# Seven-product FFN pairs added up in PSUM, with two plain tiles in place of three, and whole 128-row blocks at x

## The chip, the cores and the metric

The kernel runs on one core of a Trainium2 chip. The metric is the device time of one execution in microseconds. The kernel before has a median of 978.66 us over 3 runs (978.25 to 978.79); the profiled execution took 978.82 us, and its span, from the first to the last instruction, is 977.0 us.

## The reference

One layer of a streaming encoder on 512 prompt rows and 64 sample rows (576 rows in all, width 1024). After RMSNorm one wide projection feeds attention and retention; their merged output goes through an output projection and is added to x. Then come the FFN and a small per-layer input:

```
h = rmsnorm(x, g_ffn_pre)
f = (jax.nn.silu(h @ w_ffn_gate) * (h @ w_ffn_up)) @ w_ffn_down
x = x + rmsnorm(f, g_ffn_post)
x = x + (p @ w_ple_proj) * jax.nn.sigmoid(x @ w_ple_gate)
```

Everything is in float32. The hidden width of the FFN is 2816, which is 22 tiles of 128, called f tiles.

## The kernel before

Activations are held transposed: 128 features on the partitions, the 576 rows as columns, worked on in two halves of 288. Each float32 product is made of three matmuls in a reduced type. Every operand is split in a high part (a rounded copy, by ScalarE) and a low part (the operand less the high part, by VectorE), and PSUM adds high x high, high x low and low x high. One such `triple` (L970) is three matmuls of 128x128 by 128x288. Weights go from HBM to `raw`, ScalarE makes `whi` (function `hi`), VectorE makes `wlo` (function `lo`), and TensorE waits for `lo_ready`.

*At the start.* x arrives with its rows on the partitions, in five blocks: four of 128 rows, and one of the 64 sample rows. `x_transposes(k)` (L770) turns 128 features of all five blocks; the last transpose is of 64 rows. There are eight such groups for x, two for p, and one like it in `row_factor` (L751). Between them run the first units of the projection. ScalarE makes `xh` from PSUM, VectorE makes `xl` and the copy `x_t`.

*The FFN.* An f tile needs a gate and an up product. The first three f tiles (`PLAIN`) are plain: gate and up are units `("ffn", n)`, each of 8 k tiles and 2 halves, 96 matmuls in all for an f tile. The other 19 are *pairs*: gate and up of one f tile are the two halves of a block product done with seven products in place of eight (a Strassen-Winograd form). Each product is of 4 k tiles, so a pair has 84 matmuls. The factors on the side of the activations are parts of `yh`, `yl`, or differences of them: `t_sum` (VectorE) forms four differences of 4x288 columns, `t_high` (ScalarE, L1490) and `t_low` (VectorE, L2152) split them into `th` and `tl`. They are made once, before the first pair. The factors on the side of the weights are quarters of the loaded weights or sums of them: `sum_of` (VectorE, L2189) writes `s_sum`, then `hi` and `lo` split it. PA0, PA1, PB1 and the like name the seven products; each has a PSUM bank of its own. What comes out is added by VectorE in SBUF: `u_sums`, `gate_sum`, `up_late` and `f_out` hold seven additions of 288 columns and the final product of 576. ScalarE copies only the first product (`kept`), and does the SiLU. The function `product_out` is what ScalarE and VectorE do once product t of pair i is done; part of it is operand t of pair i+1.

*The order* is written out by hand, engine by engine: an engine does its list in order, and each step waits for counters of the others. `bank_turns` numbers the uses of each PSUM bank; `open_bank` on TensorE waits until the use before has been read (`bank_read`). Behind the first units ("ffn", 0) to ("ffn", 3) TensorE goes on with units 4 and 5, which are the third plain tile, then with the pairs. Meanwhile ScalarE and VectorE finish f of the tiles 0 and 1 (`gate_silu`, `f_half`, `f_half_low`), make the `t` factors, and with `first_products` the operands of the first pair.

Of the kernel before, what the change touches and what calls it, by code (L numbers as in the profile page):

```python
# [14 lines left out]
P = 128  # L15
# [126 lines left out]
def block_size(b):  # L142
# [4 lines left out]
    if b == RH:  # L147
# [5 lines left out]
PLAIN = 3  # L153
# [4 lines left out]
FFN_BANK = {(0, 0): 0, (1, 0): 1, (2, 0): 2, (3, 0): 3, (0, 1): 0, (1, 1): 4, (2, 1): 5, (3, 1): 1,  # L158
            (4, 0): 2, (4, 1): 3, (5, 0): 4, (5, 1): 5}
PA0, PS1, PS2, PA1, PS4, PS3, PB1 = range(PRODUCTS)  # L160
# [98 lines left out]
def bank_turns():  # L259
# [3 lines left out]
    used = [0] * PRODUCTS  # L263
    n = 0
    for e in EVENTS:
        if e[0] == "prod":
            b = e[2]
        else:
            if e in (("down", 0, 0), ("down", KD, 0), ("down", 2 * KD, 0)):
                n = 0  # L270
# [21 lines left out]
S_STEP = {PS1: 0, PS2: 1, PS4: 2, PS3: 3}  # L292


def encoder_layer(nc, x_p, x_s, p_p, p_s, cache_k, cache_v, state_in, g_mix_pre, w_in, sinks_in,
                  w_ba, w_br, w_out, g_mix_post, g_ffn_pre, w_fg, w_fu, w_fd, g_ffn_post, w_pp, w_pg,
                  table_in, scratch, y_p, y_s, k_p, v_p, r_p, k_s, v_s, r_s):
    with ExitStack() as ctx:
# [228 lines left out]
        banks = [acc[:, b // 2, b % 2, 0:HALF] for b in range(4)] + [small[:, 512 * b:512 * b + HALF] for b in range(3)]  # L527
# [161 lines left out]
        def _(pe):  # L689
# [61 lines left out]
            def row_factor(n):  # L751

                pe.wait_ge(rstd_ready, n + 1)
                for r in range(RT):
                    size = P if r < RT - 1 else DEC
                    ins = nc.tensor.transpose(small[:, r * P:r * P + size], rstd[0:size, r:r + 1].to_broadcast([size, P]),
                                              ident[0:size, 0:size])
                ins.then_inc(bcast_done, 1)
# [11 lines left out]
            def x_transposes(k):  # L770

                if k < KD:
# [6 lines left out]
                for r in range(RT):  # L779
                    size = P if r < RT - 1 else DEC  # L780
                    ins = nc.tensor.transpose(small[:, at + r * P:at + r * P + size],
                                              src[0:size, r, col:col + P], ident[0:size, 0:size])
# [191 lines left out]
            def triple(e, weights, x_h, x_l, first, last):  # L974

                (w_h, w_l), bank = weights, bank_of(e)
                nc.tensor.matmul(bank, w_h, x_h, start=first, stop=False)  # L977
                nc.tensor.matmul(bank, w_h, x_l, start=False, stop=False)  # L978
                return nc.tensor.matmul(bank, w_l, x_h, start=False, stop=last)  # L979

            def open_bank(e):
# [3 lines left out]
                elif b == PB1:  # L985
                    pe.wait_ge(yn_ready, 2 * KD)
# [108 lines left out]
            def product(i, t):  # L1095
# [7 lines left out]
                for k in range(KD // 2):  # L1103
                    ins = triple(e, weight(e, k), x_h[:, k, :], x_l[:, k, :], k == 0, k == KD // 2 - 1)
                done(ins, e)

            def f_wait(i):

                pe.wait_ge(f_lo, (3, 4, 6)[i] if i < PLAIN else PLAIN + i + 1)
# [50 lines left out]
        def _(act):  # L1160
# [344 lines left out]
            hi(("ffn", 4))  # L1505
            hi(("ffn", 5))
# [9 lines left out]
            def first_products(i, n):


                for t in ((PA0, PS1), (PS2, PA1), (PS4, PS3), (PB1,))[n]:
                    hi(("prod", i, t))  # L1520

            for n in range(3):
                first_products(PLAIN, n)
            gate_silu(2, 0)
            gate_silu(2, 1)
            first_products(PLAIN, 3)
            f_half(2, 0)
            f_half(2, 1)
# [6 lines left out]
            def f_high(i):  # L1535

                act.wait_ge(f_ready, i - PLAIN + 1)
                nc.scalar.activation(fh[:, i - GROUPS[group_of(i)][0], :], ta[:, :], ACT.Copy).then_inc(f_hi, 1)

            def product_out(i, t, first, last):  # L1540
# [11 lines left out]
                if t == PS3:  # L1552
# [113 lines left out]
        def _(dve):  # L1666
# [499 lines left out]
            lo(("ffn", 4))  # L2166
# [397 lines left out]
```

## Time and profile before

| what | value |
|---|---|
| median of 3 runs | 978.66 us |
| profiled execution | 978.82 us |
| its span | 977.0 us |
| TensorE busy | 969.8 us, 99% |
| VectorE busy | 632.0 us, 65% |
| ScalarE busy | 397.6 us, 41% |
| TensorE in the chain that ended last | 98% |
| granted TensorE clock | 1.00 |

Busy time counts an engine as working when any of its instructions runs; matmuls overlap their neighbours in the pipe, so the time from one start to the next is the cost of a matmul and not its duration. A wait row names the engine that waits, what it was about to do, and who released it.

### The profile page before, as it was taken

The numbers are of one execution on the slowest core, as the hardware profiler recorded it, in microseconds if no ns is written. First come the engines' busy times: TensorE is split into PE (matmuls) and PEld (weight loads), VectorE is DVE, ScalarE is ACT, GpSimd is POOL, SyncE is SP. The second block draws the span as 40 slices with busy tenths as digits, with TensorE's granted clock in tenths as the row PEclk, the third lists the DMA queues.
The fourth block names the chain that finished last, engine by engine and source line by source line (L and its number), as shares of the span: only waits on it lengthen the run. The fifth ranks groups of instructions, "written<-read, shape, count | busy, mean of one in ns | idle before, by whom it ended". The sixth has DMA issues, their size and how long they took to land.

```text
span 977.0 us, 18648 instructions
## 1 busy us (share of the span) xinstructions
PE 969.8 (99%) x7263; PEld 950.6 (97%) x7263; DVE 632.0 (65%) x1248; ACT 397.6 (41%) x699; POOL 85.9 (9%) x140
## 2 busy tenths in 40 slices
PE   8999999999999999999999999999999999999998
PEld 7999999999999999999999999999999999999997
DVE  5554676757665643435458899525997469976772
ACT  5333533434343522223455555424453234543352
POOL 2123212122100000010003000000000000030000
PEclk9999999999999999999999999999999999999999
DMA  8534221222122222246604533521334213356221
GB/s 216 147 110 131 80 61 55 66 76 70 58 69 66 76 88 86 76 124 174 195 4 119 205 87 87 152 65 46 109 102 122 79 44 106 105 188 207 87 55 44
DMA packets 166244, 98.67 MB, mean 101 GB/s; under 512 B 14688, under 2 KB 162560, under 8 KB 165904
## 3 DMA queue, kind: packets, MB, share of 16 engines
q1 hardware_dynamic: 159936, 79.19, 28.5%
q0 software_dynamic: 4336, 16.67, 4.9%
q10 hardware_dynamic: 1888, 1.64, 0.6%
q8 instruction: 58, 0.95, 0.4%
q14 instruction: 26, 0.21, 0.1%
HBM read 86.79 MB, written 10.75 MB: 100 GB/s over the span
## 4 chain that ended last, share of the span: by engine, by line
PE 98%; DMA 1%; DVE 0%; SPq 0%; ACT 0%; issue 0%; DVEq 0%; ACTq 0%
PE acc L697 37%; PE acc L977 11%; PE acc L978 11%; PE acc L979 11%; PE small L977 6%; PE small L978 6%; PE small L979 6%; PE small L846 1%; PE small L892 1%; PE small L863 1%; PE small L896 1%; PE small L855 1%; PE small L894 1%; DMA x_row<-in_x_sample 1%; PE acc L808 1%; PE small L877 1%
## 5 line engine op out<-in xcount | busy, mean ns | idle before, releaser
L697 PE MATMUL acc<-xh,whi 128*128 128x288 f32 x720 | 158.6, 301 | 0.1
L697 PE MATMUL acc<-xh,wlo 128*128 128x288 f32 x720 | 153.4, 294 | 0.0
L697 PE MATMUL acc<-xl,whi 128*128 128x288 f32 x720 | 153.4, 294 | 0.0
L1166 ACT ACTIVATE whi<-raw 128x1024 fp32r<-128x1024 f32 (+1 forms) x60 | 60.1, 1001 | 197.6 <-PE acc L697 196.0
L697 PEld LDWEIGHTS acc<-xh,whi 128*128 128x128 f32 x720 | 114.0, 188 | 5.8 <-issue 4.7
L697 PEld LDWEIGHTS acc<-xh,wlo 128*128 128x128 f32 x720 | 115.0, 188 | 0.0
L697 PEld LDWEIGHTS acc<-xl,whi 128*128 128x128 f32 x720 | 114.9, 188 | 0.0
L2008 DVE TENSOR_TENSOR wlo<-raw,whi 128x512 fp32r<-128x512 f32 (+2 forms) x93 | 81.0, 872 | 51.2 <-ACT whi L1387 35.5
L977 PE MATMUL acc<-yh,whi 128*128 128x288 f32 x360 | 107.0, 297 | 0.0
L979 PE MATMUL acc<-yh,wlo 128*128 128x288 f32 x360 | 106.1, 295 | 0.0
L1675 DVE TENSOR_TENSOR wlo<-raw,whi 128x1024 fp32r<-128x1024 f32 (+1 forms) x62 | 71.8, 1158 | 44.2 <-ACT whi L1166 43.4
L977 PE MATMUL acc<-fh,whi 128*128 128x288 f32 x264 | 77.9, 295 | 0.0
L978 PE MATMUL acc<-fl,whi 128*128 128x288 f32 x264 | 77.8, 295 | 0.0
L978 PE MATMUL acc<-yl,whi 128*128 128x288 f32 x264 | 77.7, 294 | 0.0
L979 PE MATMUL acc<-fh,wlo 128*128 128x288 f32 x264 | 77.7, 294 | 0.0
L1395 ACT ACTIVATE whi<-s_sum 128x512 fp32r<-128x512 f32 x76 | 47.7, 630 | 61.5 <-DVE s_sum L2189 50.9
L977 PEld LDWEIGHTS acc<-yh,whi 128*128 128x128 f32 x360 | 67.6, 188 | 0.0
L979 PEld LDWEIGHTS acc<-yh,wlo 128*128 128x128 f32 x360 | 67.6, 188 | 0.0
L1711 DVE TENSOR_TENSOR zt<-acc,rb 128x576 f32<-128x576 f32 x40 | 30.3, 756 | 52.3 <-PE acc L697 52.3
L2008 DVE TENSOR_TENSOR wlo<-s_sum,whi 128x512 fp32r<-128x512 f32 x76 | 51.7, 683 | 8.6 <-ACT whi L1395 8.6
L1387 ACT ACTIVATE whi<-raw 128x1024 fp32r<-128x1024 f32 (+1 forms) x38 | 38.2, 1011 | 40.8 <-PE acc L979 18.1
L978 PEld LDWEIGHTS acc<-yl,whi 128*128 128x128 f32 x264 | 49.6, 188 | 0.0
(337 smaller groups left out, 2392.2 us busy)
## 6 DMA issues: line engine op xcount, KB each, us to landing
raw<-in_w_in SPq DMA_DIRECT2D x91, 256.0 KB, 3.2
raw<-in_w_ffn_gate SPq DMA_DIRECT2D x44, 256.0 KB, 3.4
raw<-in_w_ffn_up SPq DMA_DIRECT2D x44, 256.0 KB, 4.1
raw<-in_w_ffn_down SPq DMA_DIRECT2D x32, 256.0 KB, 3.4
res<-x_scratch POOLq DMA_DIRECT2D x16, 288.0 KB, 4.3
raw<-in_w_branch_ret SPq DMA_DIRECT2D x16, 256.0 KB, 3.1
raw<-in_w_out SPq DMA_DIRECT2D x16, 256.0 KB, 4.3
raw<-in_w_ffn_down SPq DMA_DIRECT2D x16, 192.0 KB, 3.5
```

The lines of the kernel that those rows point to most:

```text
L697: ins = nc.tensor.matmul(acc[:, a, hf, 0:HALF], w[:, s, at:at + P], x(k)[:, hf * HALF:(hf + 1) * HALF], start=first and n == 0 and m == 0, ...
L808: ins = nc.tensor.matmul(acc[:, 0, hf, 0:HALF], w[:, at], x[:, k, hf * HALF:(hf + 1) * HALF], start=k == 0 and m == 0, stop=k == KD - 1 an ...
L846: ins = nc.tensor.matmul(att[0:nq, slot * KW + k0:slot * KW + k1], q_st[64 * g:64 * g + 64, 2 * p + j, 0:nq], k_st[64 * g:64 * g + 64, k0: ...
L977: nc.tensor.matmul(bank, w_h, x_h, start=first, stop=False)
L978: nc.tensor.matmul(bank, w_h, x_l, start=False, stop=False)
L979: return nc.tensor.matmul(bank, w_l, x_h, start=False, stop=last)
L1166: nc.scalar.activation(whi[:, s, 0:n], raw[:, s, 0:n], ACT.Copy).then_inc(hi_ready, 1)
L1387: nc.scalar.activation(dst[:, 0:n], raw_of(RAW[u])[:, 0:n], ACT.Copy).then_inc(hi_ready, 1)
L1395: nc.scalar.activation(dst[:, 0:QUART], s_sum[:, S_STEP[u[2]], :], ACT.Copy).then_inc(hi_ready, 1)
L1675: nc.vector.tensor_tensor(wlo[:, s, 0:n], raw[:, s, 0:n], whi[:, s, 0:n].bitcast(F32), ALU.subtract).then_inc(lo_ready, 1)
L1711: nc.vector.tensor_tensor(halves(dst), acc_of(a), halves(rb[:, :]), ALU.mult).then_inc(acc_free[a], 1)
L2008: nc.vector.tensor_tensor(dst[:, 0:n], src[:, 0:n], high[:, 0:n], ALU.subtract).then_inc(lo_ready, 1)
```

## The change

1. `PLAIN` is 2: f tile 2 becomes a pair, the units ("ffn", 4) and ("ffn", 5) go.
2. Within a pair, products that are summed go to one PSUM bank and are added up there: PA0, then PS2, PS3 and PB1 on top (bank 0 of the pair's three), PS1 and on top of it PS4 (bank 2), PA1 alone (bank 1). Pairs take the banks 0 to 2 and 3 to 5 in turn. What is needed of a sum on its way is copied out by ScalarE before TensorE adds the next one: PA0, PS1 and PS2. VectorE keeps three additions of 288 columns (`add_kept`), and the final product is in two pieces of 288 columns, one of them read straight from PSUM. PS3 now comes before PS4.
3. In front of the first pair, the lists of ScalarE and VectorE are set again: the first pair's operands come between the `t` factors, and with the first pair the operands of the second come two products later (`OPERANDS_AT`).
4. At x, p and the row factor, the block of 64 sample rows is transposed as a block of 128 rows, whose other rows GpSimd has set to zero.

```diff
-PLAIN = 3
+PLAIN = 2
...
-PA0, PS1, PS2, PA1, PS4, PS3, PB1 = range(PRODUCTS)
+PA0, PS1, PS2, PA1, PS3, PS4, PB1 = range(PRODUCTS)
+OPERANDS_AT = ([[t] for t in range(PRODUCTS)],
+               [[], [], [PA0], [PS1], [PS2], [PA1, PS3], [PS4, PB1]])
+PAIR_BANK = {PA0: 0, PS2: 0, PS3: 0, PB1: 0, PA1: 1, PS1: 2, PS4: 2}
+ADDED = (PS2, PS3, PB1, PS4)
...
-            b = e[2]
+            b = PAIR_BANK[e[2]] + 3 * ((e[1] + PLAIN) % 2)
...
             def x_transposes(k):
+                pe.wait_ge(rows_padded, 1 if k < KD else 2)
...
-                    size = P if r < RT - 1 else DEC
-                    ins = nc.tensor.transpose(small[:, at + r * P:at + r * P + size],
-                                              src[0:size, r, col:col + P], ident[0:size, 0:size])
+                    ins = nc.tensor.transpose(small[:, at + r * P:at + (r + 1) * P], src[:, r, col:col + P], ident)
...
-            for n in (4, 5):
-                for h in range(2):
-                    half_unit("ffn", n, h, yh, yl)
...
-                    ins = triple(e, weight(e, k), x_h[:, k, :], x_l[:, k, :], k == 0, k == KD // 2 - 1)
+                    ins = triple(e, weight(e, k), x_h[:, k, :], x_l[:, k, :], k == 0 and t not in ADDED,
+                                 k == KD // 2 - 1, t in ADDED)
...
-                if t == PA0:
-                    copy_out(e, kept[:, 0, :])
+                if t in (PA0, PS1, PS2):
+                    copy_out(e, kept[:, (PA0, PS1, PS2).index(t), :])
...
-                    hi(("prod", i + 1, t))
+                    for n in OPERANDS_AT[i == PLAIN][t]:
+                        hi(("prod", i + 1, n))
...
+            def add_kept(i, t, dst, n):
+                e, copied = ("prod", i, t), ("prod", i, (PA0, PS1, PS2)[n])
+                dve.wait_ge(bank_read[BANK[copied]], TURN[copied] + 1)
+                dve.wait_ge(pe_done, EVENT[e])
+                nc.vector.tensor_tensor(dst, bank_of(e), kept[:, n, :], ALU.add).then_inc(bank_read[BANK[e]], 1)
...
+            nc.gpsimd.memset(x_row[DEC:P, RT - 1, :], 0.0).then_inc(rows_padded, 1)
+            nc.gpsimd.memset(p_row[DEC:P, RT - 1, :], 0.0).then_inc(rows_padded, 1)
```

How the lists stand in front of the first pair is seen best in the built programs. VectorE before, from the third `t_sum` to the first pair's first low part (`wlo_128<-raw_126` at the end; `ta<-...,tb` is `f_half`, `fl` is `f_half_low`, `tl` is `t_low`, and `wlo<-raw` 128x1024 is the low part of ("ffn", 5)):

```order
L2145 TENSOR_TENSOR t_high_part<-wide 128x1152
L2141 SCALAR_TENSOR_TENSOR t_high_part<-t_low_part,wide 128x1152
L2008 TENSOR_TENSOR wlo<-raw,whi 128x1024
L2127 TENSOR_TENSOR ta<-small,tb 128x288
L2132 TENSOR_TENSOR fl<-ta,fh 128x288
L2152 TENSOR_TENSOR tl<-t_low_part,th 128x1152 x2
L2127 TENSOR_TENSOR ta<-acc,tb 128x288
L2132 TENSOR_TENSOR fl<-ta,fh 128x288
L2189 TENSOR_TENSOR s_sum<-raw_126 128x512
L2008 TENSOR_TENSOR wlo_128<-raw_126,whi_127 128x512
```

VectorE in the change, from the same step:

```order
L2140 TENSOR_TENSOR t_high_part<-wide 128x1152
L2136 SCALAR_TENSOR_TENSOR t_high_part<-t_low_part,wide 128x1152
L2122 TENSOR_TENSOR ta<-small,tb 128x288
L2127 TENSOR_TENSOR fl<-ta,fh 128x288
L2147 TENSOR_TENSOR tl<-t_low_part,th 128x1152
L2122 TENSOR_TENSOR ta<-acc,tb 128x288
L2180 TENSOR_TENSOR s_sum<-raw 128x512
L2003 TENSOR_TENSOR wlo<-raw,whi 128x512
L2180 TENSOR_TENSOR s_sum<-s_sum,raw 128x512
L2003 TENSOR_TENSOR wlo<-s_sum,whi 128x512
L2147 TENSOR_TENSOR tl<-t_low_part,th 128x1152
```

Two low parts of 1024 columns are gone (one stands just ahead of these rows), the second `tl` now comes behind the first pair's first operands, and so does a `fl`.

ScalarE before, from the first two `t_high` to the copy of the first product (`kept<-acc`); `tb` is the SiLU of a plain tile, `fh` the high part of f, `whi<-s_sum` and `whi<-raw` 128x512 are operands of the first pair:

```order
L1490 ACTIVATE th<-t_low_part 128x1152 x2
L1479 ACTIVATE tb<-small 128x288
L1485 ACTIVATE fh<-ta 128x288
L1490 ACTIVATE th<-t_high_part 128x1152 x2
L1392 ACTIVATE whi_127<-raw_126 128x512
L1395 ACTIVATE whi_127<-s_sum 128x512 x2
L1392 ACTIVATE whi_127<-raw_126 128x512
L1395 ACTIVATE whi<-s_sum 128x512 x2
L1479 ACTIVATE tb<-acc 128x288 x2
L1392 ACTIVATE whi<-raw_126 128x512
L1485 ACTIVATE fh<-ta 128x288 x2
L1533 ACTIVATE kept<-acc 128x288
```

ScalarE in the change, from the same step:

```order
L1488 ACTIVATE th<-t_low_part 128x1152 x2
L1477 ACTIVATE tb<-small 128x288
L1483 ACTIVATE fh<-ta 128x288
L1390 ACTIVATE whi<-raw 128x512
L1393 ACTIVATE whi<-s_sum 128x512
L1488 ACTIVATE th<-t_high_part 128x1152
L1393 ACTIVATE whi<-s_sum 128x512
L1390 ACTIVATE whi<-raw 128x512
L1488 ACTIVATE th<-t_high_part 128x1152
L1393 ACTIVATE whi_127<-s_sum 128x512 x2
L1390 ACTIVATE whi_127<-raw 128x512
L1525 ACTIVATE kept<-acc 128x288 x3
```

The first pair's high parts now stand between the `th` in place of behind them, and the SiLU and `fh` of the third plain tile are gone. The copy of the first product, now with those of the second and third, stands behind all seven high parts of its pair, as it did before. What is new is that TensorE waits for it: PS2 is opened by `bank_read` of the bank that the copy reads.

## Rows read from the trace of the kernel before

**Rows 1.** The profile's page, parts 1 and 4: busy time by engine; shares of the ending chain.

```profile
PE 969.8 (99%) x7263; PEld 950.6 (97%) x7263; DVE 632.0 (65%) x1248; ACT 397.6 (41%) x699; POOL 85.9 (9%) x140
...
PE 98%; DMA 1%; DVE 0%; SPq 0%; ACT 0%; issue 0%; DVEq 0%; ACTq 0%
```

**Rows 2.** The waits of TensorE: what it waited for, us in total, times, longest; first and last.

```profile
PE small L781 <- DMA x_row<-in_x_sample: 1.6, 2, 0.8
...
PE acc L764 <- DVE rowsum L1686: 1.1, 1, 1.1
```

**Rows 3.** Windows: last plain tile, first pair: length, busy (instructions) by engine, clock, DMA.

```profile
549.87:562.62 12.75, 12.75 (x98) 12.75 (x97) 9.56 (x14) 7.92 (x12) 0.00 (x0) 1.00 0.24 67
562.62:573.74 11.12, 11.12 (x86) 11.12 (x85) 10.63 (x19) 5.34 (x12) 0.00 (x0) 1.00 0.23 66
```

**Rows 4.** Timeline of VectorE before the first pair: start us, us, line, operation, count, idle before.

```profile
550.42 1.22 DVE L2008 TENSOR_TENSOR wlo<-raw,whi 128x1024 fp32r<-128x1024 f32 x1
551.56 0.45 DVE L2127 TENSOR_TENSOR ta<-small,tb 128x288 f32<-128x288 f32 x1
...
553.58 2.63 DVE L2152 TENSOR_TENSOR tl<-t_low_part,th 128x1152 fp32r<-128x1152 f32 x2 [0.60 <-ACT th L1490]
556.12 0.45 DVE L2127 TENSOR_TENSOR ta<-acc,tb 128x288 f32<-128x288 f32 x1
...
559.71 0.69 DVE L2008 TENSOR_TENSOR wlo<-raw,whi 128x512 fp32r<-128x512 f32 x1 [1.57 <-ACT whi L1392]
```

**Rows 5.** Timeline of ScalarE before the first pair, the same columns.

```profile
552.04 0.45 ACT L1485 ACTIVATE fh<-ta 128x288 fp32r<-128x288 f32 x1 [6.30 <-DVE ta L2127]
552.39 2.21 ACT L1490 ACTIVATE th<-t_low_part 128x1152 fp32r<-128x1152 f32 x2
554.50 0.39 ACT L1479 ACTIVATE tb<-small 128x288 f32<-128x288 f32 x1
556.61 0.45 ACT L1485 ACTIVATE fh<-ta 128x288 fp32r<-128x288 f32 x1 [1.71 <-DVE ta L2127]
556.96 2.20 ACT L1490 ACTIVATE th<-t_high_part 128x1152 fp32r<-128x1152 f32 x2
...
559.59 0.62 ACT L1395 ACTIVATE whi<-s_sum 128x512 fp32r<-128x512 f32 x1
...
565.82 0.41 ACT L1533 ACTIVATE kept<-acc 128x288 f32<-128x288 f32 x1
```

**Rows 6.** Timeline of TensorE's weight loads at one block of x, by form.

```profile
12.29 0.49 PEld L781 LDWEIGHTS small<-tab,x_row 128*128 128x128 f32 x4
12.95 0.14 PEld L781 LDWEIGHTS small<-tab,x_row 64*128 64x128 f32 x1 [0.17 <-issue]
```

**Rows 7.** Windows on TensorE: one block at x, and the two at p.

```profile
18.40:19.13 0.73, 0.73 (x7) 1.00 0.90 362
28.00:29.52 1.52, 1.52 (x12) 1.00 0.53 104
```

**Rows 8.** Timeline of TensorE behind the block of 18.40.

```profile
19.13 0.53 PE L697 MATMUL acc<-xh,whi 128*128 128x288 f32 x2
19.50 0.43 PE L697 MATMUL acc<-xl,whi 128*128 128x288 f32 x2
```

**Rows 9.** Timeline of ScalarE in the first projection unit.

```profile
14.30 1.06 ACT L1166 ACTIVATE whi<-raw 128x1024 fp32r<-128x1024 f32 x1 [0.29 <-DMA raw<-in_w_in]
```

**Rows 10.** Timeline of TensorE: the matmul behind that low part, and the row factor.

```profile
16.71 0.53 PE L697 MATMUL acc<-xh,whi 128*128 128x288 f32 x2
...
34.41 0.79 PE L756 MATMUL small<-tab,rstd 128*128 128x128 f32 x5
```

**Rows 11.** Timeline of GpSimd: the row factor's power.

```profile
32.72 1.21 POOL L2395 TENSOR_TENSOR rstd<-rowvar,neg_half 128x5 f32<-128x5 f32 x1 [14.03 <-DVE rowvar L1681]
```

**Rows 12.** Timeline of TensorE: the same matmul of ones at the start and later.

```profile
1.11 4.10 PE L764 MATMUL acc<-ones 128*128 128x128 f32 x20 [1.11 <-DVE rowsum L1686]
...
7.76 1.38 PE L764 MATMUL acc<-ones 128*128 128x128 f32 x10
```

More of the change, by code:

```diff
@@ L291 @@
 Y_SENT = [sum(Y_DMA[q::4]) for q in range(4)]
-S_STEP = {PS1: 0, PS2: 1, PS4: 2, PS3: 3}
+S_STEP = {PS1: 0, PS2: 1, PS3: 2, PS4: 3}
 def encoder_layer(nc, x_p, x_s, p_p, p_s, cache_k, cache_v, state_in, g_mix_pre, w_in, sinks_in,
@@ L972, in weight, with triple @@
                 return hi[:, s % 2, at:at + P], lo[:, s % 2, at:at + P]
[L974 removed]
+            def triple(e, weights, x_h, x_l, first, last, added=False):
                 (w_h, w_l), bank = weights, bank_of(e)
[L977 to L979 removed]
+                nc.tensor.matmul(bank, w_h, x_h, start=first, stop=False, skip_group_check=added)
+                nc.tensor.matmul(bank, w_h, x_l, start=False, stop=False, skip_group_check=added)
+                return nc.tensor.matmul(bank, w_l, x_h, start=False, stop=last, skip_group_check=added)
             def open_bank(e):
@@ L1512, in _, with first_products @@
             f_half(1, 1)
+            def first_products(i, n):
+                for t in ((PA0, PS1), (PS2, PA1), (PS3, PS4), (PB1,))[n]:
+                    hi(("prod", i, t))
+            first_products(PLAIN, 0)
             t_high(2)
+            first_products(PLAIN, 1)
             t_high(3)
[L1516 to L1525, printed above, removed]
+            first_products(PLAIN, 2)
             first_products(PLAIN, 3)
-            f_half(2, 0)
-            f_half(2, 1)
             def copy_out(e, dst):
@@ L2197, in product_operand @@
                 elif t == PS2:
+                    sum_of(i, PS3)
+                elif t == PA1:
                     sum_of(i, PS4)
-                elif t == PA1:
-                    sum_of(i, PS3)
                 lo(("prod", i, t))
             def first_products(i, n):
-                for t in ((PA0, PS1), (PS2, PA1), (PS4, PS3), (PB1,))[n]:
+                for t in ((PA0, PS1), (PS2, PA1), (PS3, PS4), (PB1,))[n]:
                     product_operand(i, t)
             first_products(PLAIN, 0)
+            t_low(1)
             first_products(PLAIN, 1)
-            f_half(2, 0, 4)
-            f_half(2, 1, 5)
             t_low(2)
@@ L2263, in product_out @@
             def product_out(i, t, first, last):
-                if t == PS2:
-                    u_sums(i)
+                if t == PS3:
+                    add_kept(i, PS3, up[:, cols(1)], 1)
                 elif t == PS4:
-                    gate_sum(i)
-                elif t == PS3:
-                    up_late(i)
+                    add_kept(i, PS4, zt[:, 1, cols(1)], 2)
                 elif t == PB1:
                     f_out(i)
+                if i == PLAIN and t == PS2:
+                    f_half_low(1, 1, 3)
```

71 lines of the change are left out of this document (23 added, 48 removed).

## Prediction

> **What bounds the kernel.** I read the page first: TensorE is busy 969.8 of 977.0 us, and it holds 98% of the chain that ended last [rows 1]. VectorE and ScalarE have 35% and 59% of the span free, so what they save is worth nothing by itself. Then the waits of TensorE: three rows, the first and the last of which are shown, 1.6 and 1.1 us [rows 2]: the arrival of x, the last output, the start. The kernel is one queue of matmuls, and a change counts in two ways alone: what it takes out of that queue, and where it makes the queue wait. So I read windows of the stretch that is changed, and then walked the lists of the two engines that feed it, with the durations of the timeline. The granted clock is 1.00 in both windows [rows 3].
>
> **Part 1, a plain tile becomes a pair.** The last plain tile takes 12.75 us (96 matmuls, 0.133 each), the first pair 11.12 (84) [rows 3]. PSUM adding doesn't change the count of matmuls. Gain: 12.75 - 11.12 = 1.63, taken as -1.6 us. It applies once.
>
> **Part 2, the entry to the first pair.** The tile that goes was also cover: in those 12.75 us VectorE worked 9.56 and ScalarE 7.92 [rows 3], making t factors and the first pair's operands. Now TensorE asks for the first product at 549.87, in times of the trace before. I walk both lists from there. A start is 0.03 behind what releases it (`ta` done at 552.01, `fh` at 552.04), and where nothing is waited for, an instruction starts 0.09 before the one ahead ends (551.56 against 550.42 + 1.22) [rows 4, 5].
> - VectorE: two low parts of 1024 columns are gone, each worth 1.14 (550.42 to 551.56) [rows 4]. So `ta` of tile 1, half 0 (the row of 551.56; the walk calls it f_half(0,1)) starts at 551.56 - 2.28 = 549.28.
> - ScalarE: `fh` follows it 0.48 later, 549.76; the two `th` 0.35 after that, 550.11; `tb` (SiLU) 2.11 later, 552.22, done 552.61 [rows 5]. VectorE meanwhile does one `tl` (1.35, two take 2.63) behind the first `th`, to 552.65 [rows 4].
> - VectorE: `ta` of the last plain half 552.65; ScalarE: `fh` 0.49 later, 553.14; `whi` of PA0 0.35 later, 553.49, and 0.62 long, 554.11 [rows 4, 5]. VectorE: `wlo` of PA0 554.14, 0.69 long [rows 4]. TensorE starts PA0 at 554.86. **First wait: 4.99 us.**
> - PS1 has its operand at 556.03 and starts on time, 556.45; TensorE is free for PS2 at 558.04 (a product is 11.12 / 7 = 1.59).
> - PS2 adds on PA0's bank, so ScalarE must have copied PA0, and that copy stands behind all seven high parts. ScalarE goes on: `whi` of PS1 554.01, third `th` 554.54 (1.06 each), PS2 555.60, PA1 556.14, fourth `th` 556.67. PS3's waits for its `s_sum`. VectorE: `s_sum` (taken as long as `wlo`) and `wlo` step by 0.60, `tl` by 1.27; from the `wlo` at 554.14 come s_sum, wlo, tl, then PS3's s_sum at 557.21, done 557.90; wlo, then PS4's s_sum at 558.41, done 559.10. So `whi` of PS4 starts at 559.13, that of PB1 0.54 later at 559.67, the copy at 560.20, 0.41 long [rows 5]. PS2 starts at 560.63. **Second wait: 2.59 us.**
> - PS3 needs the copy of PS2, made in PA1's 1.59 us: in time. PB1 needs VectorE's addition of PS3. Behind PB1's `wlo` at 563.35, the late `fl` and two operands of the next pair (four steps of 0.60) that is about 566.7 to 567.2, against 566.99 on TensorE. Taken as 0.15.
>
> Sum: 4.99 + 2.59 + 0.15 = 7.7 us of waiting. Below: the walk would have to be wrong at its links, and half the first wait and all of the second gone gives 2.5. Above: each of the some 20 links 0.05 longer, and PB1 late by 0.5, gives 9.
>
> **Part 3, the other pairs.** Nothing waits, by the same steps. A copy out of PSUM (0.41) must be done in one product's 1.59 us before TensorE adds on that bank; ScalarE works 5.34 of 11.12 in a pair [rows 3] and gets two copies more. VectorE, at 10.63 of 11.12 [rows 3] the tight one, loses four additions of 288 columns. The addition of PS3 has to be done while PS4 runs; the operand ahead of it is ready some 1.3 us after PA1 and the addition some 2.1, and TensorE wants the bank at 3.2. That leaves 1.1 us. If that margin were wrong by more, each of 20 pairs would pay (a rival below). From the second pair on operands are ahead, and TensorE, having waited, is later than they.
>
> **Part 4, 128-row blocks.** The weight loads of four full blocks take 0.49, so one follows the other after about 0.11; the one of 64 rows stands idle 0.17 first, though nothing was missing [rows 6]. A group of five takes 0.73 where five steps of 0.11 are 0.55, and the next two matmuls start 0.37 before the following ones in place of 0.27 [rows 7, 8]. So a change of row count costs 0.18 on the way and 0.11 behind: 0.29 for a group. The two groups at p take 1.52 against 1.09, and with the 0.11 behind that is 0.54 [rows 7]. There are eleven groups, at most 3.2 us. But the first of them wait for x (1.6 us [rows 2]), and at 14.30 ScalarE waits for weights from HBM [rows 9]: its 1.06 us and VectorE's low part of 1024 columns behind it (1.22, as in [rows 4]) fix the matmul of 16.71 [rows 10] to a landing. What was gained ahead is lost there but for about 0.05. Behind it: 0.11 of the group just ahead, two groups of 0.29, 0.54 at p, 0.29 for the row factor = 1.5 us. The row factor waits for GpSimd's power, ready at 32.72 + 1.21 = 33.93 [rows 11] against its use at 34.41 [rows 10]; its margin of 0.48 shrinks by about 0.35, because the list ahead of it hangs on the blocks at p and they move up too. I take -1.55; bounds 0 (all eaten by the loads) and -3.2. The two memsets on GpSimd have the 4 us of the first matmuls of ones [rows 12] to themselves, before x is there; queued behind them are four small loads of gains, which are asked for only behind the row factor.
>
> **Sum.** On the profiled execution: 977.0 - 1.6 - 1.55 + 7.7 = 981.5 of span, with the 1.8 around it 983.3; that execution is 0.16 above the median, which makes **983.2 us**, slower by 0.46%.
>
> A rule that speaks against the change is weighed apart. The same matmul of ones took 0.21 us at the start (20 in 4.10) and 0.14 at 7.76 (10 in 1.38, the last one's tail in it) [rows 12]: TensorE starts at the lower of its two clocks, 1.2 GHz. Its two short waits for x, 0.8 us the longest [rows 2], did not bring that back. A wait of 5 us is in no row. The Trainium skill, "TensorE: Matmul & The Clock Gate", section "What's actually happening", says that an idle TensorE falls to half its clock and regains it only after a stretch of work. By that rule the first wait would be followed by slow matmuls.
>
> **Rivals.**
> - *The clock falls in the first wait.* At 1.2 GHz for as long as at the start (some 3.3 us) PA0 and PS1 end 1.65 later, at 559.7: still ahead of PS2's 560.62, so free. For twice as long, or falling again in the second wait, up to 3.3 us of slow matmuls lie on the path, 1.65 us more. 984 to 985.
> - *Faster.* The walk is wrong: operands arrive within about a microsecond of TensorE. For it: VectorE idles 1.57 and 0.60 in this stretch and ScalarE 6.30 [rows 4, 5]. Against it: these are the links of one chain back and forth between the two, not slack. Price: 977.0 - 1.6 - 1.55 = 973.85 of span, 975.5 us. It turns faster once both waits together stay under 3.1 us.
> - *Only the first wait.* If the copy of PA0 were not behind the high parts, as the lists say it is, TensorE would lose 5.1: 980.6. On the edge of slower.
> - *A pair has a wait of its own.* 0.2 us for PB1 in 20 pairs: 4 us more, 987. Against it: VectorE's load falls.
> - *128-row blocks bring nothing or twice as much:* 984.8, or 981.6.
>
> **How the numbers follow.** The forecast of both waits near 7.7 has 0.66 (982 to 984.8); the clock 0.12; a wait in each pair 0.06; only the first wait, or waits of 3 to 5 us, 0.07; faster 0.06; near nothing 0.03. For 8 in 10 I take 981.3 to 985.6. This kernel's times tell 0.2% (2 us) from no change. Slower by more: 0.66 + 0.12 + 0.06 + some of the edge = 0.88; same 0.06; faster 0.06.
>
> **What would show it.** Two rows of waits on TensorE at the first pair: one of about 5 us for VectorE's `wlo`, one of about 2.6 for ScalarE's `kept`. No other TensorE wait from there to the last gate unit. Groups at x of 0.55 us from 18 us on, and no idle weight load there. A pair still 11.1 us. VectorE's busy share of a pair down by over 1 us with no effect. It is wrong if the first `prod` follows the plain units without a gap, or if gaps come in every pair.

## The result: 984.0 us, slower by 0.5%, and the profile after

The changed kernel takes 984.0 us (median of 6 runs, 983.8 to 984.3), the kernel before 978.7 on the same chip: ratio 1.0053 [1.0043, 1.0063]. The forecast was 983.2, slower. Its profiled execution has a span of 982.0 us against 977.0.

The page of the changed kernel, parts 1, 2 and 4 (busy by engine; granted clock in tenths over 40 slices; shares of the ending chain), against [rows 1]:

```profile
PE 968.9 (99%) x7251; PEld 950.8 (97%) x7251; DVE 610.7 (62%) x1202; ACT 414.5 (42%) x743; POOL 86.8 (9%) x142
...
PEclk9999999999999999999999899999999999999999
...
PE 93%; DVE 3%; issue 1%; DMA 1%; ACT 1%; SPq 1%; DVEq 0%; ACTq 0%
```

TensorE has 12 instructions less and VectorE 21 us less work, yet TensorE's share of the ending chain falls from 98 to 93%: others hold the end now and then. One slice, the 23rd of 40 (540 to 565 us), has a lower clock. Where, the waits of TensorE say, against [rows 2]:

```profile
PE acc L979 <- DVE wlo L2003: 4.9, 1, 4.9
PE small L784 <- DMA x_row<-in_x_sample: 1.5, 2, 1.1
...
PE acc L979 <- ACT kept L1525: 0.4, 1, 0.4
...
PE acc L979 <- DVE up L2218: 0.2, 1, 0.2
```

L979 is the first matmul of a `triple`, here that of a product. There is one wait of 4.9 us for VectorE's `wlo`, as forecast, but only 0.4 for ScalarE's `kept`, where 2.6 was forecast. The windows of the stretch, with all engines (length, busy (instructions) of PE, PEld, DVE, ACT, POOL, clock, DMA share, GB/s), against [rows 3]: the first pair with its waits, the second and the third; then the first pair's PA0, PS1 and PS2 alone.

```profile
548.10:567.25 19.15, 13.88 (x86) 13.37 (x85) 17.74 (x27) 13.11 (x22) 0.00 (x0) 0.82 0.19 55
567.25:578.77 11.52, 11.36 (x86) 11.16 (x85) 11.52 (x22) 7.28 (x14) 0.00 (x0) 1.00 0.33 94
578.77:589.90 11.13, 11.13 (x86) 11.13 (x85) 9.59 (x19) 6.85 (x14) 0.00 (x0) 1.00 0.34 96
553.12:556.16 3.04, 3.04 (x12) 3.04 (x13) 3.04 (x5) 2.89 (x4) 0.00 (x0) 0.50 0.01 3
556.16:558.47 2.31, 2.31 (x13) 2.22 (x12) 2.31 (x4) 1.67 (x3) 0.00 (x0) 0.66 0.00 0
559.03:560.69 1.66, 1.66 (x13) 1.66 (x13) 1.66 (x4) 0.15 (x1) 0.00 (x0) 1.00 0.00 0
```

- The plain units are done at 548.10 in place of 549.87 [rows 3]: 1.77 gained before the first pair.
- The first pair takes 19.15 where a pair without waits takes 11.14 (the third: 11.13). That is 8.01 lost.
- The second takes 11.52, 0.38 lost behind the 0.2 wait for `up` (an idle gap is shown from a matmul's modelled end; what is lost is counted from start to start, and behind the gap the second matmul starts 0.21 after the first in place of 0.13).
- A pair of 11.14 in place of the plain tile of 12.75: 1.61 gained.

Sum: -1.77 - 1.61 + 8.01 + 0.38 = +5.01, the 5.0 between the spans (982.0 less 977.0).

PA0 took 3.04 us at half the clock (0.50, so 1.2 GHz) and PS1 2.31 at 0.66, where a product takes 1.59 at 1.00. The clock did fall in the first wait: it is 0.50 from the first matmul of PA0 on. VectorE and ScalarE around it:

```profile
552.37 0.69 DVE L2003 TENSOR_TENSOR wlo<-raw,whi 128x512 fp32r<-128x512 f32 x1 [0.43 <-ACT whi L1390]
...
564.98 0.46 DVE L2218 TENSOR_TENSOR up<-acc,kept 128x288 f32<-128x288 f32 x1
```

```profile
557.97 0.61 ACT L1390 ACTIVATE whi<-raw 128x512 fp32r<-128x512 f32 x1
558.49 0.69 ACT L1525 ACTIVATE kept<-acc 128x288 f32<-128x288 f32 x2
```

PA0's `wlo` is ready at 553.06 and TensorE starts at 553.12. ScalarE copies PA0 and PS1 at 558.49, directly behind the last high part: the copy is late as forecast. What TensorE would have spent waiting for it, it spent on slow matmuls.

The blocks at x and p, against [rows 6 to 8]: windows of one block at x and of the two at p, and the weight loads of one block.

```profile
17.87:18.34 0.47, 0.47 (x8) 0.47 (x6) 0.47 (x2) 0.00 (x0) 0.46 (x1) 1.00 0.10 30
26.90:27.91 1.01, 1.01 (x12) 1.01 (x11) 0.26 (x1) 1.01 (x3) 0.00 (x0) 1.00 0.98 194
```

```profile
11.58 0.60 PEld L784 LDWEIGHTS small<-tab,x_row 128*128 128x128 f32 x5
```

And TensorE behind the block of 17.87, the answer to [rows 8]:

```profile
18.34 0.51 PE L702 MATMUL acc<-xh,whi 128*128 128x288 f32 x2
18.68 0.42 PE L702 MATMUL acc<-xl,whi 128*128 128x288 f32 x2
```

A block takes 0.47 where it took 0.73, the two at p 1.01 where they took 1.52, and the five loads follow one another without the idle 0.17. The matmul that waits for the late weights, at 16.71 before [rows 10], starts here at 16.18:

```profile
16.18 0.53 PE L702 MATMUL acc<-xh,whi 128*128 128x288 f32 x2 [0.42 <-DVE wlo L1670]
```

### The profile page after: what moved, and what is told of

The parts are those of the page before. It is cut to its first block, busy times and chain, and to the rows that moved or that the text cites. A ratio compares the mean times of both kernels' runs of the same rounds, so it can differ in the third digit from the quotient of the medians.

```text
span 982.0 us, 18658 instructions
## 1 busy us (share of the span) xinstructions
PE 968.9 (99%) x7251; PEld 950.8 (97%) x7251; DVE 610.7 (62%) x1202; ACT 414.5 (42%) x743; POOL 86.8 (9%) x142
## 4 chain that ended last, share of the span: by engine, by line
PE 93%; DVE 3%; issue 1%; DMA 1%; ACT 1%; SPq 1%; DVEq 0%; ACTq 0%
PE acc L702 37%; PE acc L979 12%; PE acc L980 12%; PE acc L981 12%; PE small L979 4%; PE small L980 4%; PE small L981 4%; PE small L848 1%; PE small L894 1%; PE small L865 1%; PE small L898 1%; DVE wlo L2003 1%; PE small L857 1%; PE small L896 1%; DMA raw<-in_w_in 1%
## 5 line engine op out<-in xcount | busy, mean ns | idle before, releaser
L1164 ACT ACTIVATE whi<-raw 128x1024 fp32r<-128x1024 f32 (+1 forms) x60 | 60.1, 1001 | 197.6 <-PE acc L702 196.0
L979 PE MATMUL acc<-yh,whi 128*128 128x288 f32 x352 | 105.4, 300 | 4.9 <-DVE wlo L2003 4.9
L979 PE MATMUL acc<-th,whi 128*128 128x288 f32 x280 | 83.0, 297 | 0.6 <-ACT kept L1525 0.4
L980 PE MATMUL acc<-tl,whi 128*128 128x288 f32 x280 | 82.9, 296 | 0.0
L981 PE MATMUL acc<-th,wlo 128*128 128x288 f32 x280 | 82.7, 295 | 0.0
L979 PE MATMUL acc<-fh,whi 128*128 128x288 f32 x250 | 73.9, 296 | 0.0
L980 PE MATMUL acc<-fl,whi 128*128 128x288 f32 x250 | 73.8, 295 | 0.0
L981 PE MATMUL acc<-fh,wlo 128*128 128x288 f32 x250 | 73.6, 294 | 0.0
L979 PEld LDWEIGHTS acc<-yh,whi 128*128 128x128 f32 x352 | 66.6, 189 | 5.1 <-DVE wlo L2003 5.1
L1393 ACT ACTIVATE whi<-s_sum 128x512 fp32r<-128x512 f32 x80 | 50.2, 630 | 28.9 <-PE acc L981 17.6
```

The costliest lines, as they stand in the source:

```text
L979: nc.tensor.matmul(bank, w_h, x_h, start=first, stop=False, skip_group_check=added)
L980: nc.tensor.matmul(bank, w_h, x_l, start=False, stop=False, skip_group_check=added)
L1164: nc.scalar.activation(whi[:, s, 0:n], raw[:, s, 0:n], ACT.Copy).then_inc(hi_ready, 1)
L1393: nc.scalar.activation(dst[:, 0:QUART], s_sum[:, S_STEP[u[2]], :], ACT.Copy).then_inc(hi_ready, 1)
```

## The experiments

Each kernel ran beside the kernel before on the same chip; the ratios are to it.

### The parts apart

**128-row blocks alone, in the kernel before.**

```diff
-                    size = P if r < RT - 1 else DEC
-                    ins = nc.tensor.transpose(small[:, at + r * P:at + r * P + size],
-                                              src[0:size, r, col:col + P], ident[0:size, 0:size])
+                    ins = nc.tensor.transpose(small[:, at + r * P:at + (r + 1) * P], src[:, r, col:col + P], ident)
+            nc.gpsimd.memset(x_row[DEC:P, RT - 1, :], 0.0).then_inc(rows_padded, 1)
```

> The kernel before with nothing but the 128-row blocks at x, p and the row factor. In the changed kernel TensorE reaches the end of the last plain half unit 1.77 us earlier than before (548.10 against 549.87). If all of that is the blocks, and it lasts to the end: 978.7 - 1.8 = 976.9. Forecast's own term: 977.15. Rival, the early gain is eaten by a later wait: 978.7.

977.5 us (11 runs, 976.95 to 978.0), 0.9986 [0.9977, 0.9995]; span 975.5, 1.5 less. This part is a gain of its own, near what was forecast (1.55; the expectation of 976.9 was 0.6 too low), and this kernel beats both the one before and the changed one. Only 0.23 of it is there at the matmul that waits for the late weights:

```profile
16.48 0.54 PE L698 MATMUL acc<-xh,whi 128*128 128x288 f32 x2 [0.48 <-DVE wlo L1673]
```

**Sums in PSUM and 128-row blocks, with three plain tiles.**

```diff
-PLAIN = 2
+PLAIN = 3
+            for n in (4, 5):
+                for h in range(2):
+                    half_unit("ffn", n, h, yh, yl)
...
+            for n in range(3):
+                first_products(PLAIN, n)
+            gate_silu(2, 0)
+            gate_silu(2, 1)
+            first_products(PLAIN, 3)
```

> The changed kernel with three plain tiles and the lists in front of the first pair as before the change: adding in PSUM and the 128-row blocks alone. Theory of the two lists: adding costs nothing in a pair (11.14 us as before); the first pair's PS2 waits 0.4 us for the copy of PA0, which stands behind the other work of ScalarE. 977.3. Rival, adding costs something in every pair, 0.1 us and more in each of 19: 979 or more.

982.2 us, 1.0034 [1.0022, 1.0045]: a miss by 5 us. A wait of TensorE, a window of the two products behind the longer one, and ScalarE at it:

```profile
PE acc L979 <- ACT kept L1533: 2.8, 2, 2.4
```

```profile
570.37:575.15 4.78, 4.78 (x24) 4.78 (x25) 4.38 (x9) 2.42 (x4) 0.00 (x0) 0.64 0.54 151
```

```profile
569.30 0.63 ACT L1396 ACTIVATE whi<-s_sum 128x512 fp32r<-128x512 f32 x1 [4.03 <-DVE s_sum L2192]
569.83 0.39 ACT L1533 ACTIVATE kept<-acc 128x288 f32<-128x288 f32 x1
```

TensorE wants to add PS3 on PS2's bank. The copy of PS2 stands in ScalarE's list behind a high part of the next pair, which waited 4.03 us for VectorE's `s_sum`. Behind the 2.4 us the granted clock is down: two products take 4.78 in place of 3.19. The other pairs took 11.14. So the change costs nothing in each pair, but it makes TensorE depend on how ScalarE's list stands. Whether that is all, a version with mended lists tells (the edit is shown against this run):

```diff
+VECTOR_AT = {PLAIN: [[PA0], [], [], [], [PS1, PS2], [PA1, PS3], [PS4, PB1]]}
+SCALAR_AT = {PLAIN: [[PA0], [], [], [], [PS1, PS2], [PA1, PS3], [PS4, PB1]]}
+LATER_AT = [[PA0], [], [], [], [PS1, PS2], [PA1, PS3], [PS4, PB1]]
...
             gate_silu(2, 1)
+            copy_out(("prod", PLAIN, PA0), kept[:, 0, :])
             first_products(PLAIN, 3)
...
+                if t == PS4 and i == PLAIN:
+                    copy_out(("prod", PLAIN + 1, PA0), kept[:, 0, :])
...
+                if i == PLAIN and t == PS4:
+                    f_half_low(2, 0, 4)
+                    f_half_low(2, 1, 5)
```

> Sums in PSUM and 128-row blocks with three plain tiles, as in the run before of that kind, but with ScalarE's copy of the first product ahead of the last high part, VectorE's `up` addition ahead of two operands, the low parts of f tile 2 behind it, and the second pair's operands later on both engines. Theory (adding up in PSUM costs no time in itself, it only makes TensorE wait where a copy or an addition stands late in a list): the waits of 0.4 and 2.4 and the fall of the clock go, span 975.5 and time 977.4, what the 128-row blocks alone gave (977.5). Rival (one more copy and bank hand-over per product cost something in each pair): 978.5 or more. If the waits only move to the second pair: 979 to 981.

977.7 us (11 runs), 0.9988 [0.9979, 0.9997]. TensorE waits nowhere in the FFN. Its first three pairs in windows:

```profile
561.29:572.40 11.11, 11.11 (x86) 11.11 (x85) 10.65 (x18) 6.59 (x15) 0.00 (x0) 1.00 0.24 68
572.40:583.55 11.15, 11.15 (x87) 11.15 (x85) 10.07 (x20) 6.37 (x13) 0.00 (x0) 1.00 0.43 123
583.55:594.70 11.15, 11.15 (x86) 11.15 (x85) 9.22 (x18) 6.29 (x13) 0.00 (x0) 1.00 0.35 96
```

That is the time of the 128-row blocks alone (977.5), to within the spread of the runs. Summing in PSUM is free here and worth nothing: VectorE's busy time falls from 631.7 us (blocks alone) to 601.9, and no time is gained by it. With the third plain tile kept, nothing of the loss is left; the lists were mended together, so which of these edits was needed isn't shown.

### The second wait and the clock

**The copy of the first product ahead of the last high parts** (the changed kernel otherwise).

```diff
-            first_products(PLAIN, 2)
-            first_products(PLAIN, 3)
...
+            hi(("prod", PLAIN, PS3))
+            copy_out(("prod", PLAIN, PA0), kept[:, 0, :])
+            hi(("prod", PLAIN, PS4))
+            first_products(PLAIN, 3)
```

> The changed kernel with ScalarE's copy of the first pair's PA0 placed ahead of the high parts of PS4 and PB1. Theory of the two lists: in the changed kernel's trace PS1 ends slowly at 558.5 and PS2 starts at 559.0, so the copy's place costs only 0.5 us, and that is given back: PB1 waits for VectorE's addition of PS3, which stands in its list at 564.98 to 565.44 whatever TensorE does, against PB1's start at 565.58. Gain 0.1 us: 983.9, and a TensorE wait for `up` of about 0.7 in place of those for `kept` (0.4) and `up` (0.2). Rival, the copy is a full term of the sum as in the forecast (2.6 us): 981.4.

984.0 us, 1.0054 [1.0040, 1.0068]: the same time. TensorE's waits, ScalarE's copy, and TensorE's start of PB1:

```profile
PE acc L979 <- DVE wlo L2006: 4.9, 1, 4.9
...
PE acc L979 <- DVE up L2221: 1.0, 2, 0.9
```

```profile
557.00 0.39 ACT L1523 ACTIVATE kept<-acc 128x288 f32<-128x288 f32 x1
```

```profile
565.82 0.37 PE L979 MATMUL acc<-th,whi 128*128 128x288 f32 x1 [0.86 <-DVE up L2221]
```

The copy comes 1.5 us earlier, and the wait moves to VectorE's `up`, which is no earlier than before (565.22; 564.98 in the changed kernel). PB1 starts at 565.82; in the changed kernel it is 565.58. Both are 0.24 later because this execution already came to the first pair's PA0 0.24 later (553.36 in place of 553.12).

**The same, and `up` added before the second pair's operands.**

```diff
+UP_FIRST = [[], [], [], [], [PA0, PS1, PS2], [PA1, PS3], [PS4, PB1]]
...
-                    for n in OPERANDS_AT[i == PLAIN][t]:
+                    for n in (OPERANDS_AT[0] if i > PLAIN else UP_FIRST)[t]:
```

> The changed kernel with the early copy of PA0 (as in the kernel with only that) and, on VectorE, the addition of the first pair's PS3 ahead of the second pair's first operands. Theory of the two lists: PS2 starts when the slow PS1 is done, 558.5, PB1 at 564.8 in place of 565.6. Gain 0.8 us (0.6 to 1.2): 983.2. Rival, TensorE is held by something else in the first pair (bank turns, the adding itself): no gain, 984.0.

985.2 us, 1.0066: a miss by 2 us. The second pair starts 1.2 us earlier than in the changed kernel (566.05 in place of 567.25), but has two new waits:

```profile
PE acc L980 <- ACT kept L1524: 0.8, 1, 0.8
PE acc L980 <- DVE up L2222: 0.8, 1, 0.8
```

```profile
568.01 0.69 ACT L1555 ACTIVATE tb<-zt 128x576 f32<-128x576 f32 x1 [0.70 <-DVE zt L2222]
568.61 0.64 ACT L1394 ACTIVATE whi<-s_sum 128x512 fp32r<-128x512 f32 x1
569.15 0.61 ACT L1391 ACTIVATE whi<-raw 128x512 fp32r<-128x512 f32 x1
569.66 0.39 ACT L1524 ACTIVATE kept<-acc 128x288 f32<-128x288 f32 x1
```

With the operands later, the SiLU (`tb`) and two high parts now stand ahead of the second pair's own copy. The span of the profiled execution is 982.6, 0.3 above that of the run before. The median is 1.2 above: two of the five executions took 984.4, at a mean granted clock of 0.997 and 0.998, and three 985.2 to 985.6, at 0.996. The profiled one is of the two, so no trace shows the rest.

**A filler in the first wait.** TensorE runs matmuls of ones ahead of the first pair, so that the clock has no idle time to fall in.

```diff
             several("ffn", ((2, 1), (3, 1)), yh, yl)
+            e = ("prod", PLAIN + 1, PA0)
+            pe.wait_ge(bank_read[BANK[e]], TURN[e])
+            busy(40)
```

> The changed kernel with 40 matmuls of ones (128x128, about 4.4 us, into a free bank, results unused) put on TensorE between the last plain unit and the first pair, that is in the wait of 4.9 us. The granted clock should stay at 1.00. Theory of the two lists: PA0 and PS1 take 1.6 us each in place of 3.0 and 2.2 but PS2 starts at the same 559.0, since it waits for ScalarE's copy: no change, 984.0. Rival, the lower clock is what costs: 6.8 us at half the rate are 3.4 us of lost matmuls, of which at least 1.7 come back: 982.3 or less.

984.4 us, 1.0058. The filler was too long: PA0 started at 557.39, 4.3 us later than in the changed kernel and 3.9 after its own operand was there (553.49), and the second pair started 568.63 in place of 567.25, only 1.4 us later (span 983.1 in place of 982.0). All products took 1.6 at full clock and nothing waited. Of the 4.3 us, 2.9 had been lost behind PA0 in the changed kernel, to slow matmuls or to late lists; this run doesn't tell which. The same filler with the edits of the run before:

> The same as the kernel with early copy and early addition, and in addition the 40 matmuls of ones in the first wait. Now nothing hides the clock. Theory of the two lists: PS2 starts at 556.8, held by its low part, PB1 at 563.2. Gain over the changed kernel 2.4 us, over the same kernel without the matmuls of ones 1.6: 981.6. If the granted clock had no price even then: 983.2, as without the matmuls of ones.

986.8 us, 1.0083, a miss by 5: PA0 starts at 557.14 behind the filler, so there was no wait left in the first pair to be gained back, and the two waits of 0.8 in the second pair stayed. A filler of the right length, `busy(20)`, in the changed kernel:

> The changed kernel, with a filler of 20 matmuls of ones ahead of the first pair, some 4.3 us by the 0.213 us that one took in the run with 40 of them; it should end just before the first pair's operand is there, so PA0 starts at about 553.1 as without it, but at full clock. Theory (each product's start is set by what VectorE and ScalarE have ready, and the clock's price lay in a wait that would have been there anyway): PA0 and PS1 take 1.6 each in place of 3.0 and 2.3, PS2 waits some 2.6 for ScalarE's copy in place of 0.4 and starts at 559.0 as before: 984.0. Should the clock then be lowered in this second wait, as it was after waits of 2.2 to 3.2 us in two other runs, PS2 takes about 3 and the time is up to 1.4 longer: 984.0 to 985.4. Rival (the low clock cost the kernel its 2.1 us): 981.9.

984.8 us (983.8 to 985.3), 1.0059 [1.0046, 1.0073]. Its longest wait, and windows of PS1 and PS2:

```profile
PE acc L979 <- ACT kept L1528: 2.5, 1, 2.5
```

```profile
554.90:556.50 1.60, 1.60 (x14) 1.52 (x12) 1.60 (x3) 1.39 (x3) 0.00 (x0) 1.00 0.01 5
559.11:562.13 3.02, 3.02 (x12) 3.02 (x13) 3.02 (x5) 0.16 (x1) 0.00 (x0) 0.50 0.00 0
```

PA0 starts at 553.20 and PS1 runs at full clock. Then the second wait is there in full, 2.5 us as forecast (2.59), PS2 starts at 559.11 (559.03 without the filler), and now the clock falls in this wait: PS2 takes 3.02. The low clock of the changed kernel lay in time that TensorE would have waited anyway: the rival, by which it cost 2.1 us, would have given 981.9. The times of the five executions say the same once more: one kept a mean granted clock of 1.000 and took 983.8, the time of the changed kernel (984.0), with the clock's price gone from both waits; the four at 0.997 to 0.998 took 984.8 to 985.3.

**All remedies together:** `busy(20)`, the early copy, `up` first, and in the second pair the copy of its first product ahead of the SiLU, in a slot of its own. The tables of what comes when (`VECTOR_AT`, `SCALAR_AT`) are those of the run with the lists in order of need and `up` first, below.

```diff
+            busy(20)
...
+                if t == PS4 and i == PLAIN:
+                    copy_out(("prod", PLAIN + 1, PA0), kept[:, 3, :])
                 if t == PS4:
                     for p in (PA1, PS4):
```

> The changed kernel with all the remedies together: the filler of 20 matmuls of ones, the copy of the first product ahead of the last high parts, `up` added first, and the second pair's edits as in the run with the lists in order of need. Theory: PA0 starts at 553.2 at full clock, PS2 waits about 0.9 for the copy, the second pair starts at 565.3 in place of 567.25 and the third without a wait: span 979.7, time 981.4. What is left against three plain tiles with 128-row blocks is the first wait of 5 us less the 1.8 that the smaller tile saves. Rival (VectorE's list as a whole is full; each wait taken away comes back): 983 or more. If only the clock falls in the wait of 0.9: 982.

982.1 us (6 runs), 1.0033 [1.0020, 1.0045]; the second pair starts at 565.50. Waits in the FFN:

```profile
PE acc L982 <- ACT kept L1529: 0.7, 1, 0.7
...
PE acc L982 <- DVE wlo L2014: 0.4, 1, 0.4
```

The wait of 0.4 for `wlo` is what the filler left of the first wait. With all of it 1.9 us comes back of the changed kernel's 5.3. Expected was 981.4; the second and the third pair take 11.46 and 11.33 in place of 11.14, which nobody had counted. The rest of the loss stays.

### The first wait

**The first pair's lists in order of need:** `whi` of PA0 and PS1 and `wlo` of PA0 come between the plain tiles' steps, each `t` factor where its product needs it.

```diff
             gate_silu(0, 1)
+            hi(("prod", PLAIN, PA0))
             f_half(0, 1)
+            hi(("prod", PLAIN, PS1))
+            gate_silu(1, 1)
             t_high(0)
+            f_half(1, 1)
             t_high(1)
-            gate_silu(1, 1)
-            f_half(1, 1)
...
+            f_half(0, 1, 2)
+            t_sum(0)
+            f_half_low(0, 1, 2)
+            t_sum(1)
+            lo(("prod", PLAIN, PA0))
```

> The changed kernel with the lists of ScalarE and VectorE in front of the first pair set in another order: f of tile 1 half 0 first, the high and low part of PA0 while the t factors are made, each copy out of PSUM right behind its product. Theory of the two lists: PA0 starts on time, PS1 waits 2.3 us for the first `tl`, PS2 0.9 for its low part, the rest on time; TensorE's waits sum up to 3.3 in place of 8.4, and the clock does not fall. Gain 4.7 to 5: 979.2. Rival, the waits come from the amount of work and not from its order: VectorE has 18.4 us of work from 541.8 on, and then the end of the pair moves by 1 to 2 us at most: 982.5.

985.4 us, 1.0063: a miss by 6. PA0 starts at once (548.18) and PS1 waits 2.2 for `tl`, as expected. Two things were not: the clock falls behind that wait (PS1 takes 2.87), and PB1 waits 3.2 and then takes 2.99 at the low clock:

```profile
PE acc L979 <- DVE up L2235: 3.2, 1, 3.2
PE acc L979 <- DVE tl L2157: 2.2, 1, 2.2
```

```profile
562.58 0.45 DVE L2137 TENSOR_TENSOR fl<-ta,fh 128x288 fp32r<-128x288 f32 x1
562.95 0.69 DVE L2181 TENSOR_TENSOR s_sum<-raw 128x512 f32<-128x512 f32 x1
563.55 0.68 DVE L2013 TENSOR_TENSOR wlo<-raw,whi 128x512 fp32r<-128x512 f32 x1
564.16 0.69 DVE L2181 TENSOR_TENSOR s_sum<-s_sum,raw 128x512 f32<-128x512 f32 x1
564.76 0.69 DVE L2013 TENSOR_TENSOR wlo<-s_sum,whi 128x512 fp32r<-128x512 f32 x1
565.36 0.45 DVE L2235 TENSOR_TENSOR up<-acc,kept 128x288 f32<-128x288 f32 x1
```

PS3 was done at 560.65; its addition stands behind a `fl` and four steps for the next pair. The expectation had left these out. **The same with `up` first and the second pair's edits:**

```diff
+VECTOR_AT = {PLAIN: [[], [], [], [], [PA0, PS1, PS2], [PA1, PS3], [PS4, PB1]]}
+SCALAR_AT = {PLAIN: [[], [], [PA0], [], [PS1, PS2], [PA1, PS3], [PS4, PB1]]}
...
+                if i == PLAIN and t == PS3:
+                    f_half_low(1, 1, 3)
```

> The run with the lists of the first pair in order of need, now with three edits in the lists of the second pair: VectorE adds `up` before it makes any operand of the second pair, ScalarE copies the second pair's first product (into a slot of its own) before its SiLU, and from the second pair on an `up` stands behind one operand of the next pair in place of three. Theory (list order alone made the 3.24 us wait for `up`, and with it the second fall of the clock, PB1 3.0 in place of 1.6): `up` at about 562.8, PB1 waits 0.5, no second fall, no wait in the second pair: 2.8 and 1.4 less than 985.4, 981.2; the wait of 2.24 for `tl` and the first fall stay. Rival (VectorE as a whole is full there: the wait turns up in the second or third pair): 984 to 985.

982.2 us (8 runs), 1.0031 [1.0021, 1.0042]. The wait for `up` is 0.5 and the second fall of the clock is gone; a wait of 1.0 for a copy in the second pair is what was missed. Four of the eight executions, at a mean granted clock of 0.999, took 981.3 to 982.1, about the 981.2 expected; the other four, the profiled one among them, took 982.4 to 982.7 at 0.997 to 0.998:

```profile
PE acc L982 <- DVE tl L2162: 2.2, 1, 2.2
...
PE acc L982 <- ACT kept L1524: 1.0, 1, 1.0
...
PE acc L982 <- DVE up L2240: 0.5, 1, 0.5
```

**The first pair's `s_sum` on GpSimd**, with the lists in order of need (the edit is shown against that run).

```diff
-            sum_of(PLAIN, PS1)
...
+            for n, (first, second) in enumerate(((b0, b1), (s1, a0), (a0, b0), (s2, a1))):
+                wait(pool, s_ready, n)
+                nc.gpsimd.tensor_tensor(s_sum[:, n, :], first, second, ALU.add).then_inc(s_ready, 1)
```

> The same order, and the four sums of weights of the first pair made by GpSimd, which is idle there. It takes 2.4 us from VectorE. Theory: one wait of 2.2 us for the first `tl` stays, all other go: 978.2 to 978.6. If GpSimd slows VectorE down while both work, or if its sums (four of some 1.3 us from 535.4 on) come late: 979.2 or more.

987.7 us (median of 5, of which one took 989.9 and one 3352), 1.0094: a miss by 9. GpSimd and VectorE here, then the same VectorE instructions in the changed kernel:

```profile
541.45 1.38 POOL L2516 TENSOR_TENSOR s_sum<-s_sum,raw 128x512 f32<-128x512 f32 x1
```

```profile
540.58 2.56 DVE L2073 TENSOR_TENSOR yl<-wide,yh 128x288 fp32r<-128x288 f32 x2
```

```profile
539.29 1.05 DVE L2063 TENSOR_TENSOR yl<-wide,yh 128x288 fp32r<-128x288 f32 x2
```

GpSimd takes 1.38 for what takes VectorE 0.69, and meanwhile two of VectorE's `yl` take 2.56 in place of 1.05. The instruction between the `yl` (`wide`, also 128x288, one of its inputs in PSUM) keeps its 0.50 beside GpSimd's additions. VectorE comes out of it 2.8 us later (`fl` at 543.07 in place of 540.26), and TensorE waits for `yl`, `tl` (2.6) and `up` (3.0).

## Why the prediction was right

- **Part 1**, 1.63: measured 1.61. And 12.75 us of cover went with it, which is what decides. Both versions with three plain tiles and no late copy take 977.5 and 977.7; the best two with two plain tiles take 982.1 and 982.2. Those two still wait for operands: 5 us at PA0, most of it under the filler, in the one, and 2.2 us at PS1 in the other, with slow matmuls behind it.
- **Part 2, first wait**, 4.99: measured 5.02 from start to start. The walk gave PA0 at 554.86 in times of the trace before; with the 1.77 that TensorE was ahead that is 553.09, and it is 553.12. That is the step on which the verdict rests, and it was right in its mechanism. A walk along two lists, link by link with the trace's own durations, held to 0.2 us over 18 us.
- **Second wait**, 2.59: right in its end and wrong in its row. PS2 starts at 559.03 (560.63 less 1.77 is 558.86), but the row shows 0.4. The step that was not in the sum is the rival's: the clock fell. PA0 and PS1 took 3.04 and 2.31, 2.2 us more than two products of 1.59, and they filled the wait. With the filler the row shows 2.5. The rival had said that this would be free at the price of the start's slow stretch (1.65); it was 2.2 and still free. Its other branch, a fall in the second wait, is what the filler brought about: 1.4 us on the path. The rival had 0.12 and a price of 984 to 985; the time of 984.0 lies in both ranges (982 to 984.8 was the forecast's), so the trace and the filler decide between them, not the time. The Trainium skill, "TensorE: Matmul & The Clock Gate", section "What's actually happening", says that an idle TensorE falls to half its clock, and the trace agrees in that (0.50 behind 4.9 us of waiting). What the fall costs depends on who would have been waited for.
- **PB1**, 0.15: 0.1 in the first pair. That VectorE would be behind for one pair more was missed: 0.38 in the second, where "no other TensorE wait" had been forecast.
- **Part 3**, no wait in the other pairs: right, 11.13 in the third. The margin counted there is one of VectorE's. The version with three plain tiles shows that ScalarE's copies have margins too, and that one was not looked at.
- **Part 4**, 1.55: 1.5 alone, and 1.77 in the changed kernel. The sum is near, but its two halves are not as forecast. Up to the matmul behind the late weights 0.05 was forecast; it came 0.53 earlier in the changed kernel (16.18 in place of 16.71) and 0.23 alone (16.48), where the weights landed earlier: their `whi` starts at 13.81 and 14.11 in place of 14.30 [rows 9]. Why they landed earlier isn't shown. Behind that matmul 1.5 was forecast, and 1.24 came in both kernels. There a group gives 0.26 in itself and 0.03 behind (the next two matmuls 0.34 before the following ones in place of 0.37). The forecast had split the same 0.29 as 0.18 and 0.11, with a block of 0.55 for the 0.47 measured. The 0.11 of the group just ahead did not come, and the row factor gave some 0.16 in place of 0.29, since its margin was used up: GpSimd's power is ready at 32.73 and TensorE starts at 32.88, 0.36 behind the matmuls ahead of it in place of 0.27.

In sum 0.8 us were missing: 0.38 in the second pair, 0.3 in the first, -0.2 from part 4, and the median lies 0.2 above the profiled execution instead of 0.16 below. That the error is so small is in part luck: the slow matmuls of 2.2 us were in no term and happened to lie in the second wait, and part 4 made up ahead of the late weights (0.5 more than forecast) what it lacked behind them (0.3). What stays open is whether the two lists can be set so that two plain tiles cover the entry; no version tried did it, and the order of need and the filler were not tried in one kernel.

## What to carry to other kernels

Work that looks dearer may be paying for cover: before a long stage is made shorter, walk the lists of the engines that prepare what comes behind it, from the moment at which the bottleneck will now ask. Letting the bottleneck engine do another's additions frees time that nobody waits for, and ties it to copies that stand somewhere in a list; each such copy needs its place ahead of whatever waits. And removing one wait is worth only the distance to the next late step: here the early copy alone, the early addition on top of it and the filler alone brought nothing, or a loss, and 1.9 us came only with all of them and the second pair's lists mended too.

## What the runs showed of the hardware

- The granted clock was 0.50 behind waits of TensorE of 2.2 us (L979 for `tl`), 2.4 and 2.5 (for `kept`), 3.2 and 4.9 us; it stayed at 1.00 behind those of 0.7 to 1.0 us. I had expected a fall from the 5 us alone. Behind 2.5 us a product of 12 matmuls took 3.02 in place of 1.60. In the case of 2.4 us the first eight matmuls behind the wait still ran at full speed.
- Behind waits of 2.2 to 2.5 us the fall is not certain. Mean clock and time change together between executions of one kernel: 1.000 and 983.8 us against 0.997 to 0.998 and 984.8 to 985.3 (filler of 20); spans of 979.1 to 979.6 at 1.000 in three of seven executions against 979.9 to 980.6 at 0.997 to 0.998 (sums in PSUM with three plain tiles, a wait of 2.4). Only the profiled executions have traces, so that the others had the same waits is inferred.
- A transposed block of 64 rows behind four of 128 cost 0.29 us in the group at 18 us (0.26 within, 0.03 behind); turning whole blocks took it away. Where TensorE then had to wait for something else, less of it was left.
- An addition of 128x512 on GpSimd took 1.38 us, and VectorE's subtractions of 128x288 (`yl`) beside it rose from 0.5 to 1.3 us each, while its `wide`, with an input in PSUM, kept its 0.5.
- An idle gap shown as 0.16 us cost TensorE 0.38 from start to start.
